# Attention's last dilation group: two blocks in one slot, six products apart, instead of one block every three products

## What is computed

```python
DILATED_GROUPS = ((128, 1), (512, 4), (2048, 16))     # window, dilation; 4 heads each, head size 64
SUB_BLOCK = 128
def _dilated_window_attention(q, k, v, window, dilation, slopes):
    span = window // dilation                         # 128 in every group
    # tokens with the same residue mod dilation form a subsequence, cut into blocks of 128;
    # a block of queries sees the keys of its own block and of the block before it
    scores = einsum(q, [k_prev, k]) * dh ** -0.5 - slope * distance, masked to 0 <= delta <= span
    m = scores.max(-1); p = exp(scores - m); den = p.sum(-1)
    out = (p / den) @ [v_prev, v];  lse = m + log(den)
```

## Time and profile before

| | |
|---|---|
| median of 3 runs | 1932.65 us (1930.1 to 1934.43) |
| the profiled execution | 1930.85 us |
| its span, first to last instruction | 1929.0 us |
| PE busy | 1910.6 us, 99% |
| DVE busy | 1220.3 us, 63% |
| ACT busy | 856.1 us, 44% |
| mean granted clock | 0.997 |

### The profile page before, as it was taken

One profiled execution on the slowest core, in us unless ns is written; L12 is line 12 of the kernel. 1 busy time (PEld: TensorE's weight loads), 2 busy tenths in 40 slices (PEclk: granted clock), 3 DMA queues, 4 the chain that ended last, 5 costly groups with the idle time before them and its releaser, 6 DMA issues.

```text
span 1929.0 us, 25790 instructions
## 1 busy us (share of the span) xinstructions
PE 1910.6 (99%) x9101; PEld 1525.0 (79%) x9101; DVE 1220.3 (63%) x2164; ACT 856.1 (44%) x1506; POOL 199.9 (10%) x354
## 2 busy tenths in 40 slices
PE   8999999999999999999999999999999999999998
PEld 7888888877777777777777777777788888888886
DVE  6755744456666666665686666666656576646776
ACT  3644633344555454666675455544554410012221
POOL 0122111110000000111210000000011100000000
PEclk9999999999999999999999999999999999999999
DMA  9765833342222222364773223323256688884442
GB/s 328 263 204 189 283 99 119 94 112 82 78 83 83 80 79 83 102 206 152 259 265 92 82 83 90 94 86 94 81 150 177 215 242 246 235 269 137 140 144 96
DMA packets 307054, 289.05 MB, mean 150 GB/s; under 512 B 38548, under 2 KB 255760, under 8 KB 304240
## 3 DMA queue, kind: packets, MB, share of 16 engines
q1 hardware_dynamic: 280976, 200.06, 35.6%
q0 software_dynamic: 25952, 87.35, 12.5%
HBM read 198.97 MB, written 88.38 MB: 149 GB/s over the span
## 4 chain that ended last, share of the span: by engine, by line
PE 96%; DVE 2%; issue 1%; ACT 1%; DMA 0%; SPq 0%; DVEq 0%; ACTq 0%
PE acc L1144 22%; PE acc L1149 21%; PE acc L1152 21%; PE acc L1384 3%; PE acc L1319 3%; PE acc L1376 3%; PE acc L1315 3%; PE acc L1380 3%; PE acc L1311 3%; PE score L1221 3%; PE pt_o L1230 2%; PE xb L1253 2%; DVE ada_acc L1708 1%; PE xb L1256 1%; PE xb L1208 1%
## 5 line engine op out<-in xcount | busy, mean ns | idle before, releaser
L1144 PE MATMUL acc<-t_hi,w_hi 128*128 128x512 f32 x1848 | 511.8, 399 | 1.4 <-DVE room L1688 1.3
L1149 PE MATMUL acc<-t_lo,w_hi 128*128 128x512 f32 x1848 | 495.4, 390 | 0.0
L1152 PE MATMUL acc<-t_hi,w_lo 128*128 128x512 f32 x1848 | 495.0, 390 | 0.0
L1144 PEld LDWEIGHTS acc<-t_hi,w_hi 128*128 128x128 f32 x1848 | 336.0, 188 | 89.4 <-issue 20.1
L1149 PEld LDWEIGHTS acc<-t_lo,w_hi 128*128 128x128 f32 x1848 | 346.9, 188 | 74.6
L1152 PEld LDWEIGHTS acc<-t_hi,w_lo 128*128 128x128 f32 x1848 | 346.9, 188 | 74.0
L1688 DVE TENSOR_TENSOR room<-acc,part 128x512 f32<-128x512 f32 x198 | 136.6, 690 | 208.3 <-PE acc L1152 202.9
L1465 ACT ACTIVATE part<-acc,cols 128x512 f32<-128x512 f32 x198 | 136.1, 687 | 217.4 <-PE acc L1152 216.9
L1688 DVE TENSOR_TENSOR room<-room 128x512 f32<-128x512 f32 (+3 forms) x220 | 176.0, 804 | 73.5 <-ACT room L1495 27.4
L1688 DVE TENSOR_TENSOR w_lo<-w_raw,w_hi 128x512 fp32r<-128x512 f32 x272 | 184.2, 685 | 52.0 <-ACT w_hi L1448 51.3
L1448 ACT CAST w_hi<-w_raw 128x512 fp32r<-128x512 f32 x264 | 162.5, 616 | 93.0 <-PE acc L1152 89.7
(11 more groups left out here) (237 smaller groups left out, 2075.8 us busy)
## 6 DMA issues: line engine op xcount, KB each, us to landing
w_raw<-in_w_in SPq DMA_DIRECT2D x132, 512.0 KB, 5.1
gate_d<-room POOLq DMA_DIRECT2D x64, 256.0 KB, 2.8
w_raw<-gate_d SPq DMA_DIRECT2D x32, 512.0 KB, 5.5
qk_d<-room POOLq DMA_DIRECT2D x24, 512.0 KB, 4.2
room<-qk_d SPq DMA_DIRECT2D x192, 64.0 KB, 2.1
room<-in_x SPq DMA_DIRECT2D x32, 256.0 KB, 6.6
t_raw<-tr_d SPq DMA_DIRECT2D x8, 1024.0 KB, 8.4
conv_d<-room POOLq DMA_DIRECT2D x16, 512.0 KB, 2.9
```

The costliest lines, as they stand in the source:

```text
L1144: nc.tensor.matmul(to, w_hi[:, s, k], t_hi[:, p, k], start=(first and k == 0), stop=False, skip_group_check=True)
L1149: nc.tensor.matmul(to, w_hi[:, s, k], t_lo[:, p, k], start=False, stop=False, skip_group_check=True)
L1152: mm = nc.tensor.matmul(to, w_lo[:, s, k], t_hi[:, p, k], start=False, stop=(last and k == KH - 1), skip_group_check=True)
```

## The change

Steps are renumbered as slots. The first 64 slots (dilations 1 and 4) stay one step each. The 32 steps of dilation 16 become 16 slots of two neighbouring blocks each, six products apart, so that there are 80 slots and not 96. A wide slot uses, for its second block, the places that the keys, probabilities and values of the block ahead have elsewhere. Its loads are one DMA of 128 KB each for q, k and v; the v load moves to the next slot's loads, and the store is one DMA as well. The last slot ends at product 421 and not at 424, and `STAT` moves with it.

```diff
+NONE = NPAIR // 3 * 2 * NBLK
+NSLOT = NONE + (NSTEP - NONE) // 2
 ATT_AT = []
-for k in range(NSTEP + 2):
-    slot = ATT_AT[-1] + 3 if k else ATT0
+for k in range(NSLOT + 2):
+    slot = ATT_AT[-1] + (6 if NONE < k < NSLOT else 3) if k else ATT0
     ATT_AT.append(PAUSE[1] if PAUSE[0] <= slot < PAUSE[1] else slot)
...
+def two(j):
+    return j >= NONE
...
                 def load_att(k):
...
+                    if k > NONE:
+                        j = k - 1
+                        sp.wait_ge(pv_done, j - 1)
+                        tj, first = step_of(j)
+                        sp.dma_start(v_ring[:, 2 * (j % 2):2 * (j % 2) + 2],
+                                     vt_d[tj, first:first + 2].rearrange("b i f -> i b f")).then_inc(att_in[k % 2], 16)
...
                     if k:
                         sp.wait_ge(scored, k)
+                    if two(k):
+                        for n, ring in enumerate((q_ring, k_ring)):
+                            sp.dma_start(ring.rearrange("p a i -> p (a i)"),
+                                         qk_d[n, t, :, blk * P:(blk + 2) * P]).then_inc(att_in[k % 2], 16)
+                        return
...
                 def scores(k):
-                    pe.wait_ge(att_in[k % 2], 48 * (k // 2 + 1))
+                    pe.wait_ge(att_in[k % 2], att_loads(k))
...
+                        if two(k):
+                            for s in range(2):
+                                mm = nc.tensor.matmul(sc_ps[:, h, s * P:(s + 1) * P], q_ring[rows_h, s], k_ring[rows_h, s],
+                                                      start=True, stop=True)
+                            continue
...
                 def turn_probs(k):
-                        for half in range(2 if has_prev(k) else 1):
+                        for half in range(2 if wide(k) else 1):
...
                 def weigh_values(k):
+                        if two(k):
+                            for s in range(2):
+                                mm = nc.tensor.matmul(xb[cols_h, s * P:(s + 1) * P], v_ring[:, 2 * (k % 2) + s, cols_h],
+                                                      prob_t[:, h, s * P:(s + 1) * P], start=True, stop=True)
...
                 def soften(k):
+                    for s, h in [(s, h) for s in range(2) for h in range(2)] if two(k) else []:
+                        o, b = slice(s * P, (s + 1) * P), slice(blk + s, blk + s + 1)
+                        ex = nc.scalar.activation(prob[:, h, o], prob[:, h, o], ACT.Exp, bias=all_m[:, t, h, b],
+                                                  scale=SCALE, accum_out=all_d[:, t, h, b])
...
                 def bias_max(k):
+                    if two(k):
+                        for s, h in [(s, h) for s in range(2) for h in range(2)]:
+                            o = slice(s * P, (s + 1) * P)
+                            own_t.up(nc.vector.tensor_tensor_reduce(
+                                out=prob[:, h, o], in0=sc_ps[:, h, o], in1=bm[:, h, P:2 * P], scale=1.0,
+                                scalar=-3.0e38, op0=ALU.add, op1=ALU.max, accum_out=all_m[:, t, h, blk + s:blk + s + 1]))
...
                 def take_o(k):
+                    if two(k):
+                        for r in range(2):
+                            dve.wait_ge(att_out[r], 16 * len(range(r, k, 2)))
+                        nc.vector.tensor_copy(att_o, xb[:, 0:2 * P].rearrange("p (a i) -> p a i", i=P)).then_inc(o_ready, 1)
+                        return
...
                 def store_att(k):
+                    if two(k):
+                        pool.dma_start(att_d[t, blk:blk + 2].rearrange("b p i -> p b i"), att_o).then_inc(att_out[k % 2], 16)
```

More of the change, by code:

```diff
@@ L168, with step_of, has_prev, wide @@
 LAST = NTT - 1
-def step_of(k):
+def two(j):
+    return j >= NONE
+def step_of(j):
+    k = NONE + 2 * (j - NONE) if two(j) else j
     return k // NBLK, k % NBLK
-def has_prev(k):
-    t, blk = step_of(k)
+def has_prev(j):
+    t, blk = step_of(j)
     return (t // 2 == 0 and blk > 0) or (t // 2 == 1 and blk % 4 > 0)
+def wide(j):
+    return two(j) or has_prev(j)
+def att_loads(j):
+    return sum({NONE: 32, NSLOT: 16}.get(i, 48) for i in range(j % 2, j + 1, 2))
 class Tally:
@@ L698, in load_att @@
                 def load_att(k):
-                    t, blk = step_of(k)
+                    t, blk = step_of(min(k, NSLOT - 1))
                     if k == 0:
                         sp.wait_ge(t_lo_done, 2 * NP + T_MORE)
-                    if k % NBLK == 0 and t % 2 == 0:
+                    if k > NONE:
[4 more added lines that the diff above has]
+                                     vt_d[tj, first:first + 2].rearrange("b i f -> i b f")).then_inc(att_in[k % 2], 16)
+                    if k == NSLOT:
+                        return
+                    if blk == 0 and t % 2 == 0:
                         for g in QKV:
@@ L757, in load_mix @@
                             sp.wait_ge(wg_out, 16)
+                            for r in range(2):
+                                sp.wait_ge(att_out[r], 16 * NSLOT // 2)
                         else:
@@ L845, in _ @@
                                 load_t(ph, p)
-                    if m + 2 in ATT_AT[:NSTEP]:
+                    if m + 2 in ATT_AT[:NSLOT + 1]:
                         load_att(ATT_AT.index(m + 2))
@@ L996, in store_att @@
                     pool.wait_ge(o_ready, k + 1)
-                    pool.dma_start(att_d[t, blk], att_o[:, k % 2]).then_inc(att_out[k % 2], 16)
+                    if two(k):
+                        pool.dma_start(att_d[t, blk:blk + 2].rearrange("b p i -> p b i"), att_o).then_inc(att_out[k % 2], 16)
+                    else:
+                        pool.dma_start(att_d[t, blk], att_o[:, k % 2]).then_inc(att_out[k % 2], 16)
                 def store_cv(g):
@@ L1245, in weigh_values @@
                         pe.wait_ge(o_ready, k)
-                    pe.wait_ge(att_in[k % 2], 48 * (k // 2 + 1))
+                    if two(k):
+                        pe.wait_ge(att_in[(k + 1) % 2], att_loads(k + 1))
+                    else:
+                        pe.wait_ge(att_in[k % 2], att_loads(k))
                     for h in range(2):
                         cols_h = slice(h * HEAD, (h + 1) * HEAD)
-                        if has_prev(k):
+                        if two(k):
+                            for s in range(2):
+                                mm = nc.tensor.matmul(xb[cols_h, s * P:(s + 1) * P], v_ring[:, 2 * (k % 2) + s, cols_h],
+                                                      prob_t[:, h, s * P:(s + 1) * P], start=True, stop=True)
+                        elif has_prev(k):
                             for half in range(2):
@@ L1268, in turn_stats @@
                 def turn_stats():
-                    pe.wait_ge(o_ready, NSTEP)
+                    pe.wait_ge(o_ready, NSLOT)
                     for w, a in enumerate((all_m, all_d)):
@@ L1350, in _ @@
                             weigh_values(k - 2)
-                        if 1 <= k <= NSTEP:
+                        if 1 <= k <= NSLOT:
                             turn_probs(k - 1)
-                        if k < NSTEP:
+                        if k < NSLOT:
                             scores(k)
@@ L1531, in soften @@
                     act.wait_ge(max_ready, k + 1)
-                    for h in range(2):
+                    for s, h in [(s, h) for s in range(2) for h in range(2)] if two(k) else []:
+                        o, b = slice(s * P, (s + 1) * P), slice(blk + s, blk + s + 1)
+                        ex = nc.scalar.activation(prob[:, h, o], prob[:, h, o], ACT.Exp, bias=all_m[:, t, h, b],
+                                                  scale=SCALE, accum_out=all_d[:, t, h, b])
+                    for h in range(0 if two(k) else 2):
                         ex = nc.scalar.activation(prob[:, h, 0:w], prob[:, h, 0:w], ACT.Exp, bias=all_m[:, t, h, blk:blk + 1],
@@ L1537, in copy_probs @@
                 def copy_probs(k):
-                    w = 2 * P if has_prev(k) else P
+                    w = 2 * P if wide(k) else P
                     act.wait_ge(turned, k + 1)
@@ L1611, in _ @@
                             za_sigmoid(g, 3)
-                    if m - 2 in ATT_AT[:NSTEP]:
+                    if m - 2 in ATT_AT[:NSLOT]:
                         soften(ATT_AT.index(m - 2))
-                    if m - 1 in ATT_AT[1:NSTEP + 1]:
+                    if m - 1 in ATT_AT[1:NSLOT + 1]:
                         copy_probs(ATT_AT.index(m - 1) - 1)
@@ L1945, in bias_max @@
                         dve.wait_ge(turned, k)
+                    if two(k):
[4 more added lines that the diff above has]
+                                scalar=-3.0e38, op0=ALU.add, op1=ALU.max, accum_out=all_m[:, t, h, blk + s:blk + s + 1]))
+                        own_t.wait()
+                        nc.vector.tensor_scalar(all_m[:, t, :, blk:blk + 2], all_m[:, t, :, blk:blk + 2], -SCALE, None,
```

(4 more changed lines are left out.)

## The result

The changed kernel takes 1919.43 us (median of 4 runs, 1918.7 to 1920.0), the one before 1931.89 (median of 4). The ratio is 0.9936, with a 95% interval of 0.9924 to 0.9947: 12.5 us faster. Forecast were 1920.9 us and a gain of 11.8, in a range of 1917.5 to 1925.5. The forecast started from 1932.65, the median of three runs of the kernel before; a fourth run moved that median to 1931.89.

The account below looks back on a forecast made before the run. PE's own instruction stream was taken as the bound. Two narrow slots (2.80 us) become one wide (2.06), saving 0.74 us 16 times, 11.8 in all: 1932.65 - 11.8 = 1920.9 us, range 1917.5 to 1925.5.

Parts of the forecast that it names:

- 16 x 0.74 = 11.8 us: Dilation 16: one wide slot costs 2.06 us, two narrow ones 2.80; 0.74 saved per pair, 16 pairs.
- The chances of the cases that gain: Whole kernel: forecast 0.79, rival 1 0.12, rival 2 0.05; faster was given as 0.95.
- the 0.75 us: Attention slot on PE: fixed cost paid per slot whatever it holds, spread around four changes of operand shape.
- 128 more columns for each head add 0.22, which is two times 0.11, so they run one after the other: Scores of a wide slot: the two heads' matmuls were taken to run serially, ruling out 0.53 us.
- the merged scores: Wide slot's four score matmuls of 128 columns: 0.42 + 0.22 = 0.64 us taken, dear end 0.84.
- The cheap end: Scores of a wide slot: heads side by side, 0.53 us; slot 1.95, 13.6 us saved in all.
- the first score pitch within a head is 0.21: Scores in the trace after: a pitch of 0.21 us would show the prediction wrong.
- rival 1: Scores of wide slots: exposed same-row weight loads at 0.21 and not 0.11; saved 8.6 us, 1924.1; chance 0.12.
- The sum of the bursts on ACT: Behind wide slots: exponentials 0.80 plus maxima 0.42 make 1.22 us, inside 1.51 us slack before place 2.
- even at twice the 2.0 us they are there: q and k loads of wide slots: issued 5.4 us ahead, so landing in 4.0 us is in time.
- Rivals 2 to 4: Dilation 16: PE waits (1925, chance 0.05); table changes, 4.0 us slower (0.02); fixed part not PE's, no change (0.02).
- rival 2: Wide slots near a place 0: PE waits up to 1 us at 5 of 16, some 1925; chance 0.05.

Follow-up runs that it names:

- split (two interruptions): Changed kernel with values and transposes put behind the product before in 14 of 16 wide slots, scores staying; 1920.16 us, ratio 0.9941.
- by block: Changed kernel with values and transposes alternating by block (both heads together) in 14 wide slots; 1922.9 us, ratio 0.9956.
- by head: Changed kernel with values and transposes alternating by head in 14 wide slots; 1929.32 us, ratio 0.999.
- transposes first: Order transposes, values, scores in all slots, instead of values, transposes, scores; 1907.86 us on the changed kernel, 1918.47 us on the kernel before.
- full-width values: On the changed kernel with transposes first, values take all 128 columns of v as weights; 1931.88 us, ratio 1.0002.
- all full: On top of full-width values, scores contract over all 128 rows with zero-padded q tiles; merged 1934.89 us, not merged 1935.26 us.
- the two full-width expectations: Full-width values expected some 1893, measured 1931.88 us; all full, merged, expected some 1859, measured 1934.89 us.
- the last two runs: Changed kernel with values and transposes alternating in 14 wide slots: by head 1929.32 us, by block 1922.9 us.
- three apart: Changed kernel with its wide slots three products apart and not six, statistics left at product 423; 1922.71 us, ratio 0.9952.

## Why the prediction was right

**The bound and the size.** PE's own stream set the time, no wait of PE grew by more than 0.1 us, and 16 x 0.74 = 11.8 us were there to 0.2 us. The slot came out at 2.06 as summed, its parts within 0.02 us. The median of 1919.43 lies 1.5 under the forecast, which is within the spread of the runs. (The chances of the cases that gain add up to 0.96, not 0.95.)

**Where the 0.75 us lie.** With 0.109 us a transpose, 0.218 for two half-array matmuls side by side, 0.218 for one that has no partner and 0.222 for each full-array one, the matmuls of a slot can be taken off its cost:

| kernel, slot | changes | cost | matmuls | rest |
|---|---|---|---|---|
| before, narrow | 4 | 1.40 | 0.65 | 0.75 |
| after, wide | 4 | 2.06 | 1.31 | 0.75 |
| split (two interruptions), wide | 4 | 2.11 | 1.31 | 0.80 |
| by block, wide | 6 | 2.37 | 1.31 | 1.06 |
| by head, wide | 6 | 2.79 | 1.74 | 1.05 |
| transposes first, narrow / wide | 3 | 1.28 / 1.95 | 0.65 / 1.31 | 0.63 / 0.64 |
| full-width values, wide | 2 | 2.22 | 1.76 | 0.46 |
| all full, narrow / wide | 0 | 1.17 / 2.28 | 1.11 / 2.21 | 0.06 / 0.07 |

The rest follows the number of shape changes at 0.11 to 0.2 us each, with 0.06 us left for the interruption; it doesn't follow the work in the slot. So the change gained by 64 shape changes fewer. The prediction had named this place from the spread of the starts alone, and the runs show it. What in a change of shape costs the time, rows, columns or the reload, stays open.

**A step that was wrong without harm.** "128 more columns for each head add 0.22, which is two times 0.11, so they run one after the other" is false. They run side by side in two passes each, which gives the same 0.22. The record at 1324.81 is both heads' second pass and not the second head's start. For the merged scores both readings give 0.64, so that this term came out right by luck. The cheap end fell to the same error: the heads do run side by side, and yet the scores take 0.65 and not 0.53. And the sign "the first score pitch within a head is 0.21" could not have told rival 1 from the forecast, as the first two pairs of records stand 0.21 us apart in the narrow slot and in the wide one. It did harm as soon as an experiment changed the shapes: the two full-width expectations failed by 39 and 76 us on it, and the slot by head rose by 0.73 us where 0.37 was expected.

**The cover.** The sum of the bursts on ACT, 1.22 us against 1.51, was not what held. Where the slots fall did. The loads are the cover that nearly failed, and no rival names them: "even at twice the 2.0 us they are there" left out the loads of the weights, and in one slot they came 0.04 us after the time at which their scores could have started.

**The rivals.** Rival 1 is refuted. The Trainium skill's rule that a weight load is hidden only behind a matmul on other rows ("TensorE: Matmul & The Clock Gate", section "Part 3: Packing small matmuls — row/col tiling") doesn't hold here: within a head, on the same 64 rows, score records follow 0.11 us apart, and in the kernel by head the value records of one head, with new weights on the same 128 rows, follow at 0.109. The same section's other rule, that matmuls on different parts of the array run at once, does hold, by the last two runs: 0.37 against 0.59 us. Rivals 2 to 4 did not occur: no wait of PE for ACT or DVE was new at six apart. The price of rival 2 was not measured on ACT; at three apart it was a load that came late.

## What to carry to other kernels

Where PE is the bound, count how often small matmuls change the operand shape against the stream and against each other. Group the work so that each shape is entered once, put the part that has the stream's own shape next to the stream, and keep matmuls on different halves of the array together: widening them to the full array to save a change costs more than the change. Before costing a matmul from the distance of two records, find out which records belong to one instruction. And before trusting a load's median time to landing, look at what else is in flight when it is issued.

## What was not expected of the hardware

- A plain 32-bit matmul of 128 columns is two passes of 0.11 us; two on different halves of the array share them, even when another matmul stands between them in the program (block 0 and block 1 of head 0 come ahead of head 1, and yet the records stand in pairs 0.013 us apart; that these are the two heads is inferred from the kernels by head and by block).
- Going between a 128x128 transpose and the stream's 128x128 matmuls is free although the number format changes; every other change costs 0.11 to 0.2 us.
- Putting one call ahead of another was worth as much as the change of this study: 13 us by itself (1918.47 us), 11.6 us on top of the change (1907.86 us).
- A 128 KB load landed after 2.4 us alone and after 4.3 us with a 512 KB load in flight.
- A wait of 2.2 us cost 3.8, as the granted clock was 0.50 for some 3 us behind it (three apart, from 1182.5 us on).
